# Homes of the rounded halves numbered by split unit, with roundings and differences one unit further ahead in an expert stage

## The reference, cut to what matters

```python
def ffn(args):
    xb, e = args
    return (jax.nn.silu(xb @ w1[e]) * (xb @ w3[e])) @ w2[e]
```

## Time and profile before

| | us |
|---|---|
| three runs | 2132.72, 2134.13, 2134.97 (median 2134.13) |
| the profiled execution, its own time | 2134.49 |
| its span, from the first to the last instruction | 2132.7 |
| granted TensorE clock, mean | 0.995 |
| PE busy, in all | 2049.1 |
| DVE busy | 1555.0 |
| ACT busy | 1192.5 |
| difference of a unit on DVE (L801), mean | 2.286 |
| rounding of a unit on ACT (L641), mean | 1.912 |

### The profile page before, as it was taken

How to read it: one execution, slowest core, us unless ns; L and a number is a source line. 1 busy time by engine, 2 the same in 40 slices (tenths; PEclk the granted TensorE clock), 3 DMA queues, 4 the chain that set the end, 5 groups by cost and what they waited for, 6 DMA issues and landing times.

```text
span 2132.7 us, 27841 instructions
## 1 busy us (share of the span) xinstructions
PE 2049.1 (96%) x10774; PEld 1669.2 (78%) x10774; DVE 1555.0 (73%) x1498; ACT 1192.5 (56%) x967; POOL 135.7 (6%) x92
## 2 busy tenths in 40 slices
PE   8999999999999999999999999999999999999996
PEld 8998888899999998887887767667777666766663
DVE  7656664453646375454769999999999999999987
ACT  5445653333333323334346777777777777777773
POOL 1000000000000000001000111011110111011010
PEclk9999999999999999999999999999999999999998
DMA  6554335655454544667779999999999999999993
GB/s 215 158 140 158 118 119 185 209 181 170 147 177 146 169 157 155 220 216 256 227 286 366 410 426 427 426 427 427 424 426 426 420 422 422 417 415 421 410 426 159
DMA packets 143693, 613.47 MB, mean 288 GB/s; under 512 B 19057, under 2 KB 31489, under 8 KB 116257
## 3 DMA queue, kind: packets, MB, share of 16 engines
q1 hardware_dynamic: 137760, 601.14, 73.2%
q0 software_dynamic: 5856, 11.26, 1.5%
HBM read 612.87 MB, written 24.13 MB: 299 GB/s over the span
## 4 chain that ended last, share of the span: by engine, by line
PE 64%; DMA 12%; DVE 11%; issue 8%; ACT 3%; POOL 1%; POOLq 0%; DVEq 0%; ACTq 0%
PE ps L2023 18%; PE ps L2004 15%; DMA raw<-in_w_dram 7%; DVE wl L801 6%; PE ps L1152 5%; PE ps L1153 5%; DMA xrows<-xscr,rowno 4%; PE ps L2381 4%; PE ps L1149 4%; ACT wh L641 2%; DVE yall L973 2%; PE ps L2136 2%; PE ps L1174 1%; PE ps L2096 1%; PE ps L2109 1%
## 5 line engine op out<-in xcount | busy, mean ns | idle before, releaser
L801 DVE TENSOR_TENSOR wl<-raw,wh 128x2048 fp32r<-128x2048 f32 x320 | 720.4, 2286 | 72.0 <-ACT wh L641 71.0
L641 ACT ACTIVATE wh<-raw 128x2048 fp32r<-128x2048 f32 x320 | 604.4, 1912 | 184.6 <-PE ps L1153 82.0
L1578 DVE TENSOR_TENSOR wl<-raw,wh 128x2048 fp32r<-128x2048 f32 (+1 forms) x168 | 379.7, 2263 | 286.5 <-ACT wh L1382 286.4
L1382 ACT ACTIVATE wh<-raw 128x2048 fp32r<-128x2048 f32 (+1 forms) x168 | 317.9, 1894 | 447.4 <-DMA raw<-in_w_in_dram 276.4
L1152 PE MATMUL ps<-wh,xg 128*128 128x512 f32 x776 | 329.8, 425 | 33.7 <-DVE wl L801 33.4
L1153 PE MATMUL ps<-wl,xg 128*128 128x512 f32 x776 | 303.7, 391 | 0.0
L2004 PE MATMUL ps<-hth,wh 128*128 128x272 f32 (+1 forms) x896 | 259.7, 290 | 3.2 <-DVE wl L1578 1.8
L2004 PE MATMUL ps<-htl,wh 128*128 128x272 f32 (+1 forms) x896 | 255.8, 285 | 0.0
L2004 PE MATMUL ps<-hth,wl 128*128 128x272 f32 (+1 forms) x896 | 255.5, 285 | 0.0
L1149 PE MATMUL ps<-raw,xg 128*128 128x512 f32 x496 | 222.9, 592 | 0.0
L1152 PEld LDWEIGHTS ps<-wh,xg 128*128 128x128 f32 x776 | 145.9, 188 | 86.0 <-DVE wl L801 38.3
(11 more groups left out here) (369 smaller groups left out, 2918.0 us busy)
## 6 DMA issues: line engine op xcount, KB each, us to landing
raw<-in_w_dram SPq DMA_DIRECT2D x192, 2048.0 KB, 16.9
raw<-in_w_in_dram SPq DMA_DIRECT2D x103, 1024.0 KB, 5.1
raw<-in_w_pa_dram SPq DMA_DIRECT2D x16, 1024.0 KB, 5.0
raw<-in_w_pb_dram SPq DMA_DIRECT2D x16, 1024.0 KB, 5.1
raw<-in_w_out_dram SPq DMA_DIRECT2D x16, 1024.0 KB, 5.1
raw<-in_w_ukv_dram SPq DMA_DIRECT2D x8, 1024.0 KB, 5.4
yscr<-zeros SPq DMA_DIRECT2D x4, 1024.0 KB, 8.4
yrow<-yscr SPq DMA_DIRECT2D x4, 1024.0 KB, 19.6
```

The lines of the kernel that those rows point to most:

```text
L641: nc.scalar.activation(wh2[:, x % HELD, :], raw_of(turn, x), ACT.Copy).then_inc(s_wh2, 1)
L801: nc.vector.tensor_tensor(wl_of(turn, x), raw_of(turn, x), wh2[:, x % HELD, :].bitcast(F32), ALU.subtract).then_inc(s_wl2, 1)
L1382: nc.scalar.activation(wh[:, n % RING1, 0:c], raw1[:, n % RING1, 0:c], ACT.Copy).then_inc(s_wh, 1)
L1578: nc.vector.tensor_tensor(wl[:, n % RING1, 0:c], raw1[:, n % RING1, 0:c], wh[:, n % RING1, 0:c].bitcast(F32), ALU.subtract).then_inc(s_wl, 1)
```

## The change

The homes are given by the number of a unit among the split ones, and a unit's rounding and difference stand beside the split unit that is 4 split units ahead of it in the count. Nothing is added or removed: the same 320 roundings and 320 differences are made.

```diff
+        SPLITS = [x for x in range(24) if x not in XR]
...
+        def shifted(x, by):
+
+            n = len(SPLITS) * (x // 24) + X_SPLIT[x % 24] + by
+            return 24 * (n // len(SPLITS)) + SPLITS[n % len(SPLITS)]
+
+        def held(x):
+            return wh2[:, X_SPLIT[x % 24] % HELD, :]
...
             def hi(turn, x):
-                if whole(turn, x):
-                    return
                 landed2(act, turn, x)
-                if isinstance(turn, int) and 24 * turn + x <= HELD:
+                if isinstance(turn, int) and split_units(turn, x) < HELD:
                     act.wait_ge(s_wused, N_UNITS)
                 else:
-                    done(act, turn, x - HELD)
-                nc.scalar.activation(wh2[:, x % HELD, :], raw_of(turn, x), ACT.Copy).then_inc(s_wh2, 1)
+                    done(act, turn, shifted(x, -HELD))
+                nc.scalar.activation(held(x), raw_of(turn, x), ACT.Copy).then_inc(s_wh2, 1)
...
-                    if x + HELD != HELD or not early:
-                        hi(turn, x + HELD)
+                    if not whole(turn, x) and not (last and x == 19):
+                        hi(turn, shifted(x, HELD))
...
-                    lo(turn, x + HELD)
+                    if not whole(turn, x) and not (last and x == 19):
+                        lo(turn, shifted(x, HELD))
```

More of the change, by code:

```diff
@@ L797, in lo @@
             def lo(turn, x):
-                if whole(turn, x):
-                    return
                 dve.wait_ge(s_wh2, split_units(turn, x) + 1)
-                nc.vector.tensor_tensor(wl_of(turn, x), raw_of(turn, x), wh2[:, x % HELD, :].bitcast(F32),
+                nc.vector.tensor_tensor(wl_of(turn, x), raw_of(turn, x), held(x).bitcast(F32),
                                         ALU.subtract).then_inc(s_wl2, 1)
@@ L1151, in unit @@
                     else:
-                        nc.tensor.matmul(o, s, wh2[:, x % HELD, c:c + 512], start=st, stop=False, skip_group_check=True)
+                        nc.tensor.matmul(o, s, held(x)[:, c:c + 512], start=st, stop=False, skip_group_check=True)
                         m = nc.tensor.matmul(o, s, wl_of(turn, x)[:, c:c + 512], start=False, stop=sp_,
```

## The result

| | kernel before | changed kernel |
|---|---|---|
| median of the runs, us | 2133.49 (4 runs, 2132.72 to 2134.97) | 2151.48 (4 runs, 2147.94 to 2153.71) |
| profiled execution, us | 2134.49 | 2147.94 |
| its span, us | 2132.7 | 2146.1 |
| granted TensorE clock, mean | 0.995 | 0.983 |

The ratio is 1.0082, with a 95% interval of 1.0068 to 1.0097: the change costs 18.0 us. I had forecast 2137.4 us and a range of 2132.5 to 2142.5 us. The forecast is wrong, and the range with it. The profiled execution of the changed kernel is the fastest of its four, so that its trace shows less than the medians: counted from the first matmul of unit 0 to the last matmul of the experts it is 15.2 us longer than that of the kernel before.

What follows compares the result with a forecast made beforehand. The prediction took the expert loads, at 61.4 us a turn with full DMA queues, as the bound over compute's 60.3. Terms of 2.6, 0 and 0.7 gave +3.3 us, a median of 2137.4 us, range 2132.5 to 2142.5.

Steps and rivals of the forecast that it cites:

- the ring: Compute chain from turn to turn through the gathered rows: 60.3 us, forecast 60.8, hidden under the loads' 61.4.
- Term 1: First turn of the expert stage: steps PE waits for fall behind differences on DVE, +2.6 us, bounds 0 to 4.2.
- Step (c): First turn behind `mix`: `hidden` falls behind two differences, so the first `w2` unit and the loads come 2.6 us later.
- nothing is regained: First turn, behind the first `w2` unit: PE stays in step with busy DVE up to unit 17, keeping the +2.6 us.
- Term 2: Steady turns: `output_rest` 0.5 us later, PE's waits move to the gathered rows, the loads hide it, 0 us.
- Term 3: Behind the last landing: the last expert's `copy_up` and `mix` come later, +0.7 us, bounds -1 to +1.2.
- R1: Steady turns: `output_rest` late by a whole 2.2 us difference, ring 62.2 us, 0.8 over the loads; 2148 us, chance 0.15.
- R2: Change pays: PE's 34.4 us of waits go, 2100 us; small form, a faster first turn, 2132 us; chance 0.10.
- R3: Nothing seen: the first turn's delay falls into gaps of other traffic, tail as before; 2134 to 2135 us, chance 0.17.

Runs made afterwards that it cites:

- e3: Kernel before with only the new numbering of homes; each rounding and difference stands where it stood. 2134.41 us, ratio 1.0003.
- e8: e2 with six idle matmuls ahead of the mix's wait in all turns but the first and last. 2141.67 us, ratio 1.0033.
- e6: e3 with the change's order of roundings and differences in the first turn only. 2142.45 us, ratio 1.0037.
- e1: Changed kernel with ten idle matmuls ahead of the wait for gathered rows in each turn but the first. 2142.87 us, ratio 1.0049.
- e4: e3 with the even expert's outputs and `output_rest` moved behind the rounding and difference of unit 20. 2148.45 us, ratio 1.0068.
- e5: e4 with ten idle matmuls ahead of the wait for gathered rows, as in e1. 2137.28 us, ratio 1.0017.
- e7: e3 with the change's order in the last turn only. 2134.91 us, ratio 1.0004.
- e10: Changed kernel with the first turn's gather matrix, combination weights and selection put back ahead of differences; rows still late. 2152.83 us, ratio 1.0089.
- e9: e2 with the first turn's gather matrix, combination weights and selection put back ahead of differences. 2138.98 us, ratio 1.0024.
- e2: Changed kernel with the even expert's outputs and `output_rest` put back ahead of the rounding and difference of unit 20. 2141.52 us, ratio 1.0037.
- e12: Changed kernel with idle matmuls ahead of three kinds of wait: gathered rows, first mix, last mix. 2139.10 us, ratio 1.0023.
- e11: e6 with seven idle matmuls ahead of the first turn's mix and twelve ahead of the second turn's rows. 2138.77 us, ratio 1.0022.

## Why the prediction was wrong, point by point

**What bounds the kernel: right in its two paces, wrong in the margin.** The loads take 61.4 us a turn and the ring 60.3. e3 and e8 show the loads' bound from the other side: 2 us less in the ring, or seven falls fewer, and the same time. But I let the queue be full from 1190 us on, from two loads, an early and a late one. The loads in between (13.0 us from issue to landing at the median in the window from 1252.9, 18.8 in the one from 1799.9) show that it fills bit by bit. Up to turn 9 the turns took some 60.3 us and the ring set the pace. From turn 1 to 15 the 14 turns took 849.3 us, 60.7 a turn. A ring longer than that costs even when it is under the 61.4 of the late turns: as an estimate, the margin was 0.4 us and not 1.1.

**Term 1, the first turn: the steps right, the size wrong.** `number_rows` was to start at 1135.45, 12.6 us behind the first matmul of the stage; it started at 1133.85, 12.7 us behind. `mix` was to start 30.7 us behind it, at the end of `select`; it started 31.1 us behind:

```profile
1133.85 0.58 PE L1132 MATMUL ps<-tokm,pg 128*128 128x1 f32 x4 [1.60 <-DVE pg L865]
...
1152.24 2.68 PE L1180 MATMUL ps<-fold,ab 128*128 128x64 f32 x16 [1.74 <-DVE wdc L929]
...
1159.95 0.49 PE L1158 MATMUL ps<-wh,hx 128*128 128x512 f32 x1
```

Step (c) is the first that fails. It let the delay of 2.1 us pass through `mix` unchanged, at the durations of the earlier trace rows. The mix ran at the lower clock, and so did the unit behind it, and the first `w2` unit started 38.8 us behind the stage's start and not 36.8. It did not wait for `hidden`, as the working had it, which had ended 1.3 us before (1158.22 + 0.42 = 1158.64). Then the step "nothing is regained" was too mild: PE also waited for the rows in the second turn, as in each later one, in e6 3.4 us with a second fall behind it. The load of the earlier trace rows went out 55.2 us behind the start (at 1176.3) instead of 50.2, so 5.0 us late and not 2.6, and it took 10.4 us to land and not 7.3. That such a delay adds in full since the loads can't make it up held: e6 is 8.0 us late to its end. The bounds of 0 to 4.2 us left both clock falls out.

**Term 2, the steady turns: this is the step that cost the forecast.** I had `output_rest` 0.5 us later in a ring of 60.8 us, and PE's waits moved to the gathered rows, "some 2.5 us a turn". They did, 2.9 us a turn (40.7 us in 14, after 10.3 before), and the sum of PE's waits remained, as forecast. The order's own part was even less than 0.5: 41.5 us from landing to `output_rest` in e1, 41.4 before. What the working lacked is that a wait of this length at one place isn't the same as the same time in small waits: the clock falls, and transposes and a unit take 1.6 us more. This 1.6 stands in the ring. The step that failed is "60.3 + 0.5 = 60.8 us is still under the 61.4 of the loads, which hide it": the ring was 61.9 us in the early turns, 61.6 on average (862.5 us in 14), against the 60.7 that the kernel before took, and nothing hid it. That is 13.2 us. e4 against e5 measures what the falls do, 14.5 us late and 2.8 us. With the falls covered, e1 takes 60.4 us in the early turns and loses 1.5 us from turn 1 to 15 (850.8 after 849.3), so that the forecast of a hidden order holds but for the falls. The working read the clock column of the earlier trace rows as a constant, though by its own forecast the wait for the rows was to more than double.

**Term 3, the end: right in its place, small in its effect.** `mix` was to come 5.5 us before the last landing; it came at 2093.38, with the landing at 2081.1 + 17.7 = 2098.8, so 5.4 us. The clock falls there too, and PE's last matmul of the experts started 12.7 us behind the landing (2111.5) and not 10.5 (2098.1 behind 2087.6). That is 2.2 us more, and the term had 0.7. Alone, in e7, the last turn cost 0.4 us, less than can be measured, so the order of the last turn by itself doesn't give the 2.2; what does is open.

**The rivals.** R1 gave 2148 us and named the place where the time went, at 0.15. Its mechanism was another: `output_rest` was not late by a whole difference. Its point of decision, 1.1 us of growth in the ring, was set against the loads' 61.4 and not against the 60.7 that the turns took on average. That its 0.8 us in 14 turns lies so near to the 0.9 measured is luck. R2 failed as argued: the 34.4 us of PE's waits for differences went, and the time grew. R3 fell with term 1.

**The sum.** The terms don't add up as I had them add. Alone, the late outputs cost 14.5 us, the first turn 8.0 and the last 0.4, 22.9 in all; together they cost 18.0, and e10, with a first turn 2.8 us shorter and no time gained, points to a first turn that is partly hidden then. Which part of that is scatter of the falls' length and which is the ring is not settled.

## What to carry to other kernels

Before moving work so that several small waits of TensorE become one longer wait, price the matmuls behind it at both clock levels, and ask whether they stand in the ring that sets the pace. If one long wait can't be avoided, a few idle matmuls in front of it, written into memory that is overwritten anyway, gave back 11.7 us of 14.5 here, and a faster ring or fewer falls in front of a queue of loads that is full gave nothing. A full queue late in a stage doesn't tell that it was full early: follow the time from issue to landing from turn to turn before taking a ring's growth as hidden. A delay in the first turn was paid in full here.

## What the runs showed of the hardware

- The granted clock fell from 1.00 to 0.50 (2.4 to 1.2 GHz) behind waits of 2.4 to 3.5 us in a stream of matmuls, in each of 13 turns of the changed kernel, and was back at 1.00 after 3.4 to 6.8 us.
- The length of a gap alone doesn't tell. The clock stayed at 1.00 behind 2.9 us in turn 1 of the changed kernel and behind 3.12 us in e10, and fell with 3.15 us in the same place in e9. Behind gaps of 1.8 us it stayed at 1.00 in the kernel before and fell in e6.
- In e2 it fell at 7 of 14 mixes, those with gaps of 1.1 to 2.1 us in front (at the others it was 0.7 us at most). The gaps were followed by 16 matmuls of 128x64 and 8 of one or two columns, and PE counts as busy in those. In e12 it fell behind two mixes that had waited only 0.2 to 0.3 us.
- With 1.7 us of idle matmuls of 128x128 in a gap of some 1.9 us it stayed at 1.00 (e11).
- The mean clock of a kernel says little: 0.983 went with 18.0 us late in the changed kernel, and 0.984 with 7.6 us in e2, where e8 shows that the steady turns' falls cost nothing.
